# Two models' blocks on one core: modulation pieces in the index and softmax stretches, projection pieces alone beside stick-breaking, a picking product, four buffers beside near attention

## The chip, the cores and the metric

One core of a Trainium2 chip runs the whole program. The metric is the device time of one execution in microseconds. The kernel before took 2896.35 us, the median of three runs (2890.53 to 2899.73).

## The reference

Two stacks of two layers each run one after the other on 256 tokens of width 1024, all in fp32. The first stack has in each layer a gated feed-forward, a mixer of three attentions (forgetting, stick-breaking, sparse with an index) and a second feed-forward:

```python
(q_a, k_a, v_a, f_a, q_b, k_b, v_b, q_c, c_kv, q_i, k_i, w_i, gates) = jnp.split(h @ w_in, _split_points(), axis=-1)
...
merged = (g_a * (y_a.reshape(B, S, W_FOX) @ w_up_fox)
          + g_b * (y_b.reshape(B, S, W_SB) @ w_up_sb)
          + g_c * (y_c.reshape(B, S, W_DSA) @ w_up_dsa))
return merged @ w_out
```

The second stack is modulated: for each layer a vector of nine times 1024 numbers is computed from a condition `c`, and one from `c_ctx`, and shifts, scales and gates the sublayers.

```python
def adaln(cond, w, b):
    m = jax.nn.silu(cond) @ w + b
    return m.reshape(m.shape[:-1] + (N_MOD, D_MODEL))
```

Its layer 0 has neighbourhood attention ("near" in the kernel) of 8 heads over 256 tokens and 256 context tokens, its layer 1 a short convolution. The modulation needs nothing but the conditions and 2 x 1024 x 9216 weights (`mod_w`, 75 MB), so it can be computed at any time before the second stack.

## The kernel before

The program is a list of phases that every engine walks through in the same order. Weights come in units of 1 MB into a ring of three buffers `raw`; ACT copies each to `whi` in a reduced format (L415), DVE subtracts to get the rest `wlo` (L428, for some units GpSimd takes 896 of 2048 columns, L670), and TensorE (PE) makes three products for each block: `whi` x `HThi`, `whi` x `HTlo`, `wlo` x `HThi`.

In a layer of the first stack the mixer runs as the phases prepare, latent, turn_index, index (top-k rounds on DVE), softmax (22 items, one for each head and block of queries) and stick (5 heads, a chain through all engines: scores z, logs, sums acc, weights, values pv). Their own work leaves engines idle, and so other work is laid beside it, cut in pieces (class `Beside`, L444). A string `BESIDE` (L42) gives the order of the pieces and `PACE` (L44) how many each phase does at each of its calls of `beside.go`. Every engine walks through the same string and does its share of each piece:

- D, a quarter of a weight unit of the remaining projections of `w_in`: on PE 6 matmuls of 512 columns (`part`, L737); on ACT the split of a later unit, and for the last D of a group of eight two evacuations (L1139, copy or tanh); on DVE, at each fourth D, the `wlo` split of a unit two ahead (L1428).
- m, 256 columns of the modulation: SP loads 1 MB of `mod_w` as two halves (L601), PE makes 8 matmuls with the 32 columns of `CT` (both conditions 16 times over) as weights into four strips of 32 partitions of one bank (`mod`, L752), DVE copies the 128 x 256 sums to `mrow` (L1432).
- t, the turn of that row: PE transposes `mrow` in two blocks (L763), DVE adds the four strips (L1440) and the bias and writes `modc` (L1441).

The two halves land in two buffers, halves of the tile `C`, so a half may be loaded when the previous row's same half has been used (`s_mod_used`). In the first stack sums and turn share bank 5, so m waits until DVE has read the previous turn (`row_read`). Beside near attention (16 items of 512 columns, phase near) the banks are 6 and 7. Of the 72 rows, 26 are computed in each of the two layers of the first stack and 20 beside near.

The stick phase on PE, with the calls of pieces after each head's step:

```python
for h in range(HS + 2):
    if h < HS:
        z(h)
    if 1 <= h <= HS:
        acc(h - 1)
    if h >= 2:
        pv(h - 2)
    beside.go(beside.pace["stick"])
```

Of the kernel before, what the change touches and what calls it, by code (L numbers as in the profile page):

```python
# [6 lines left out]
ALU = mybir.AluOpType  # L7
# [34 lines left out]
BESIDE = ("mDDDDDDDDt" * 4 + "mDtDmDtDmDtDmDtD" * 5 + "mDtDmDDDtDDD",) * 2 + ("m" + "tm" * 19 + "t",)  # L42

PACE = (dict(prepare=8, latent=(4, 2), turn_index=3, index=(4, 4, 4, 4, 4, 3), softmax=4, item=(2,), stick=6),) * 2 + (dict(item=(2, 2, 3)),)  # L44
# [7 lines left out]
def constants():  # L52
# [11 lines left out]
    add("ident", np.eye(P))  # L64
    add("upto", i[:, None] <= i[None, :])
# [40 lines left out]
def program(nc, t, out):  # L106
    with ExitStack() as ctx:
# [31 lines left out]
        mraw = C[:].rearrange("p b (c n) -> p b c n", c=4)  # L139
# [77 lines left out]
        def pieces(order, w=None, groups=()):  # L217

            out, part, groups = [], 0, iter(groups)
            for what in order:  # L220
# [10 lines left out]
                elif what == "m":  # L231
                    layer, column = next(mods)
                    out.append(("mod", len(mod_units)))
                    mod_units.extend(kn(t["mod_w_2"][layer], 4 * half, 4, column, MOD) for half in range(2))
                else:
                    out.append(("turn", layer, column // P))
            return out

        for l in range(DEPTH):
# [5 lines left out]
            def projected(n0, n1, *more):  # L245
# [7 lines left out]
            phase("beside", first=len(units), pieces=pieces(BESIDE[l], w, later), pace=PACE[l], end=len(units), banks=(5, 5),  # L253
                  after=0 if l == 0 else c_read)
# [31 lines left out]
        for l in range(DEPTH):  # L286
# [6 lines left out]
            if l == 0:  # L293
# [10 lines left out]
                phase("beside", first=len(units), pieces=pieces(BESIDE[2]), pace=PACE[2], end=len(units), banks=(6, 7), after=c_read)  # L304
# [24 lines left out]
        s_mod, s_mod_used = [sem(f"mod_landed{h}") for h in range(2)], sem("mod_used")  # L329
# [239 lines left out]
        four = small[:, 494:498].rearrange("p (k s) -> p k s", s=2)  # L569
# [6 lines left out]
        def _(sp):  # L576
# [24 lines left out]
            def load_mod(m):  # L601
                if m >= 2:
                    sp.wait_ge(s_mod_used, m - 1)
                sp.dma_start(mraw[:, m % 2], mod_units[m]).then_inc(s_mod[m % 2], 16)
# [15 lines left out]
            for ph in phases:  # L620
# [19 lines left out]
                elif ph["kind"] == "beside":  # L640
# [4 lines left out]
                    for what, m, *p in ph["pieces"]:  # L645
                        if what == "part" and p[1] == 0:
                            begin(m + 2)
                        elif what == "mod":
                            load_mod(m)
# [52 lines left out]
        def _(pe):  # L702
# [49 lines left out]
            def mod(m):  # L752
# [3 lines left out]
                for half in range(2):  # L756
                    pe.wait_ge(s_mod[half], 16 * (m // 2 + 1))
                    for c in range(4):
                        i = mm(ps[32 * c:32 * c + 32, total, 0:MOD], CT[:, 4 * half + c, :], mraw[:, half, c, :],
# [3 lines left out]
            def turn_row(l, k0):  # L763
# [3 lines left out]
                for k in range(MOD // P):  # L767
                    i = nc.tensor.transpose(ps[:, turned, k * P:(k + 1) * P], mrow[:, k * P:(k + 1) * P], ident)  # L768
# [1059 lines left out]
```

## Time and profile before

| | |
|---|---|
| median of 3 runs | 2896.35 us |
| the profiled execution, its time | 2887.4 us |
| its span (first to last instruction) | 2885.6 us |
| PE busy | 2668.5 us, 92% |
| DVE, ACT busy | 1417.5 us (49%), 1174.3 us (41%) |
| DMA | 496.16 MB, mean 172 GB/s |
| mean granted clock of TensorE | 0.952 of 2.4 GHz |

The profile is of one execution. Busy time of PE is a modelled span of pipelined matmuls. A granted clock of 1.00 is 2.4 GHz, 0.50 is 1.2 GHz. A wait names the engine and line that released it. Some fp32 matmul instructions of the program stand as two in the trace; transposes stand as one.

### The profile page before, as it was taken

Reading aid. Unit: us, or ns where it says so; the run is one execution under the profiler, and the core shown is the slowest. Engines: PE = TensorE matmul, PEld = TensorE weight load, DVE = VectorE, ACT = ScalarE, POOL = GpSimd, SP = SyncE. Lnnn points to the kernel's source line nnn. Section 1 sums busy time; section 2 is a strip of 40 time slices with the busy share of each in tenths; the row PEclk is TensorE's granted clock in tenths of the full one; section 3 lists DMA queues with packets and bytes.
Section 4 is the critical chain, followed back from the end, with each engine's and each line's share of the span. In section 5 each row is a group of like instructions: output and inputs, shape, how many; then the busy total and the mean of one; then the engine's idle time right before and its main releaser. Section 6 shows DMA issues by size and latency. Waiting matters only on the chain.

```text
span 2885.6 us, 34246 instructions
## 1 busy us (share of the span) xinstructions
PE 2668.5 (92%) x12829; PEld 2112.8 (73%) x12829; DVE 1417.5 (49%) x1830; ACT 1174.3 (41%) x1356; POOL 111.4 (4%) x85
## 2 busy tenths in 40 slices
PE   7998988899999898889989989978889999998998
PEld 6886655688788765568878878865567878876786
DVE  4555334645555633465554455543335455455554
ACT  4435333444443433444443443443024444444433
POOL 0002110000000211000000000020000000000000
PEclk9999999999999999999989999987789999998999
DMA  6555564465555656455545545562454545554453
GB/s 210 189 163 198 175 208 157 151 194 184 168 183 178 200 175 196 160 177 191 187 134 187 189 141 184 185 146 97 157 173 162 187 155 192 187 166 131 157 188 114
DMA packets 367783, 496.16 MB, mean 172 GB/s; under 512 B 14478, under 2 KB 295338, under 8 KB 367562
## 3 DMA queue, kind: packets, MB, share of 16 engines
q1 hardware_dynamic: 365338, 487.99, 51.8%
q0 software_dynamic: 2064, 5.84, 1.1%
q8 instruction: 64, 1.05, 0.1%
q10 hardware_dynamic: 288, 1.05, 0.1%
q14 instruction: 29, 0.24, 0.0%
HBM read 493.77 MB, written 1.05 MB: 171 GB/s over the span
## 4 chain that ended last, share of the span: by engine, by line
PE 84%; DVE 7%; ACT 4%; DMA 3%; issue 1%; DVEq 0%; ACTq 0%; SPq 0%; PEldq 0%
PE ps L706 79%; PE ps L786 2%; DVE wlo L428 2%; PE ps L905 2%; DMA C<-in_mod_w_dram 1%; ACT whi L415 1%; DMA raw<-in_even_w_in_dram 1%; PE ps L793 1%; PE ps L768 1%; ACT L1315 0%; DVE arena L1469 0%; DMA raw<-in_even_w_out_dram 0%; DVEq L348 0%; ACT work L1156 0%; PE ps L876 0%
## 5 line engine op out<-in xcount | busy, mean ns | idle before, releaser
L428 DVE TENSOR_TENSOR wlo<-raw,whi 128x2048 fp32r<-128x2048 f32 (+5 forms) x405 | 872.0, 2155 | 606.7 <-ACT whi L415 604.5
L706 PE MATMUL ps<-whi,HThi 128*128 128x512 f32 (+2 forms) x2360 | 958.1, 406 | 38.6 <-DVE HTlo L1475 16.9
L415 ACT ACTIVATE whi<-raw 128x2048 fp32r<-128x2048 f32 (+4 forms) x405 | 752.7, 1861 | 467.1 <-PE ps L706 432.8
L706 PE MATMUL ps<-whi,HTlo 128*128 128x512 f32 (+2 forms) x2360 | 932.8, 395 | 0.0
L706 PE MATMUL ps<-wlo,HThi 128*128 128x512 f32 (+2 forms) x2360 | 932.8, 395 | 0.0
L706 PEld LDWEIGHTS ps<-whi,HThi 128*128 128x128 f32 x2360 | 452.6, 192 | 162.5 <-issue 50.8
L706 PEld LDWEIGHTS ps<-wlo,HThi 128*128 128x128 f32 x2360 | 452.6, 192 | 96.9
L706 PEld LDWEIGHTS ps<-whi,HTlo 128*128 128x128 f32 x2360 | 453.5, 192 | 85.4
L706 PE MATMUL ps<-whi,AThi 128*128 128x512 f32 x792 | 310.0, 391 | 1.1
L706 PE MATMUL ps<-wlo,AThi 128*128 128x512 f32 x792 | 308.5, 390 | 0.0
L706 PE MATMUL ps<-whi,ATlo 128*128 128x512 f32 x792 | 308.2, 389 | 0.0
L1225 ACT ACTIVATE AThi<-ps 128x512 fp32r<-128x512 f32 x99 | 59.1, 597 | 291.9 <-PE ps L905 291.9
L706 PEld LDWEIGHTS ps<-whi,AThi 128*128 128x128 f32 x792 | 148.7, 188 | 34.9 <-issue 4.7
L706 PEld LDWEIGHTS ps<-wlo,AThi 128*128 128x128 f32 x792 | 148.6, 188 | 31.1
L706 PEld LDWEIGHTS ps<-whi,ATlo 128*128 128x128 f32 x792 | 148.7, 188 | 30.2
L1537 DVE TENSOR_TENSOR ATlo<-ps,AThi 128x512 fp32r<-128x512 f32 x99 | 68.4, 691 | 155.5 <-ACT AThi L1225 155.5
L706 PE MATMUL ps<-C,CT 128*32 128x256 f32 x1152 | 95.5, 453 | 42.6 <-DVE modc L1441 26.7
L1132 ACT ACTIVATE work<-ps,small 128x128 f32<-128x128 f32 (+2 forms) x60 | 29.5, 492 | 219.7 <-DVE small L1391 219.5
L1221 ACT ACTIVATE arena<-ps 128x256 f32<-128x256 f32 x110 | 36.2, 381 | 186.5 <-PE ps L706 186.5
L670 POOL TENSOR_TENSOR wlo<-raw,whi 128x896 fp32r<-128x896 f32 x36 | 84.0, 2333 | 390.6 <-ACT whi L415 390.6
L1221 ACT ACTIVATE arena<-ps,small 128x256 f32<-128x256 f32 x88 | 36.9, 470 | 140.8 <-PE ps L706 140.7
L1390 DVE TENSOR_REDUCE small<-ps 128x1 f32<-128x128 f32 (+2 forms) x60 | 26.8, 447 | 133.5 <-PE ps L786 87.8
(191 smaller groups left out, 1593.0 us busy)
## 6 DMA issues: line engine op xcount, KB each, us to landing
raw<-in_ffn_w_dram SPq DMA_DIRECT2D x330, 512.0 KB, 4.2
raw<-in_w_ffn_gu_dram SPq DMA_DIRECT2D x176, 512.0 KB, 4.6
C<-in_mod_w_dram SPq DMA_DIRECT2D x144, 512.0 KB, 4.3
raw<-in_w_ffn_down_dram SPq DMA_DIRECT2D x88, 512.0 KB, 4.0
raw<-in_w_in_dram SPq DMA_DIRECT2D x40, 1024.0 KB, 7.3
raw<-in_even_w_in_dram SPq DMA_DIRECT2D x12, 1024.0 KB, 5.1
raw<-in_conv_w_in_dram SPq DMA_DIRECT2D x12, 1024.0 KB, 5.1
raw<-in_w_out_dram SPq DMA_DIRECT2D x8, 1024.0 KB, 5.0
```

The source lines that it names most:

```text
L415: i = nc.scalar.activation(whi[0:rows, r, a:b], raw[0:rows, r, a:b], ACT.Copy)
L428: i = nc.vector.tensor_tensor(wlo[0:rows, r, a:b], raw[0:rows, r, a:b], whi[0:rows, r, a:b].bitcast(F32), ALU.subtract)
L670: nc.gpsimd.tensor_tensor(wlo[at], raw[at], whi[at].bitcast(F32), ALU.subtract).then_inc(s_lo_pool, 1)
L706: return nc.tensor.matmul(o, lhsT, rhs, start=first, stop=last)
L768: i = nc.tensor.transpose(ps[:, turned, k * P:(k + 1) * P], mrow[:, k * P:(k + 1) * P], ident)
L786: i = nc.tensor.matmul(S[:, o:o + ow], lh, rh, start=False, stop=j == len(mine) - 1)
L793: i = nc.tensor.transpose(T[:, c * P:(c + 1) * P], prob[(n - 1) % 2][:, c * P:(c + 1) * P], ident)
L905: i = nc.tensor.transpose(ps[:, 2, c * SEQ + b * P:c * SEQ + (b + 1) * P], av[:, b, c * P:(c + 1) * P], ident)
L1132: A(prob[n % 2][:, 0:it["n"]], ps[:, n % 2, 0:it["n"]], ACT.Exp, bias=nmx[:, n:n + 1], scale=SCALE, accum_out=rsum[:, n:n + 1]).then_inc(s ...
L1221: A(sg[:, b, :], ps[:, b, 0:GW], ACT.Silu, scale=scale).then_inc(sem("ffn_silu"), 1)
L1225: A(AT[own][0][:], ps[:, 2, :].rearrange("p (c t) -> p c t", c=2), ACT.Copy).then_inc(sem("ffn_act_hi"), 1)
L1537: V.tensor_tensor(AT[own][1][:], ps[:, 2, :].rearrange("p (c t) -> p c t", c=2), AT[own][0][:].bitcast(F32), ALU.subtract).then_inc(sem("f ...
```

## The change

`BESIDE` becomes `PROJECT + GATE`: up to the end of the index phase 32 D, 9 m and 9 t (before 32, 4 and 4, then two D, an m and a t ahead of the first item, now three D, an m and a t), in the 24 steps of softmax 24 D, 16 m, 16 t (before 24, 12, 12), and in stick 21 D alone (before 22 D, 9 m, 9 t). The turn is no longer two transposes but two products of `mrow` as weights with a constant of two columns, `pick`, which has a one in column s at the rows s of each strip of 32. They add the strips on PE and leave 4 columns, so that DVE only adds the bias, and reads 4 columns of PSUM. Beside near, four buffers are used in turn, two of them in `arena` where the matrices of the pooling branch lie until the phase near_turn is over: SP waits for that phase on PE before it loads them (`late`). Three pieces (m, t, m) come ahead of the first near item, and then two to each item.

```diff
@@ -39,9 +39,11 @@
 PJ_LATER = ((902, 1414), (1414, 1926), (390, 902), (0, 390))
-BESIDE = ("mDDDDDDDDt" * 4 + "mDtDmDtDmDtDmDtD" * 5 + "mDtDmDDDtDDD",) * 2 + ("m" + "tm" * 19 + "t",)
-
-PACE = (dict(prepare=8, latent=(4, 2), turn_index=3, index=(4, 4, 4, 4, 4, 3), softmax=4, item=(2,), stick=6),) * 2 + (dict(item=(2, 2, 3)),)
+PROJECT = "DDDDDDDm" + "tDDm" + "DD" + "tDm" + "tDDDm" * 6 + "tDD"
+GATE = "mDtDD" + "mDtDmtD" * 8 + "D" * 21
+BESIDE = (PROJECT + GATE,) * 2 + ("mtm" + "tm" * 18 + "t",)
+
+PACE = (dict(prepare=8, latent=(4, 2), turn_index=3, index=(5, 5, 5, 5, 5, 8), softmax=5, item=(2, 3, 2), stick=3),) * 2 + (dict(near=3, item=(2,)),)
 MOD = 256
@@ -62,6 +64,7 @@
     add("ident", np.eye(P))
+    add("pick", i[:, None] % 32 == np.arange(2)[None, :])
     add("upto", i[:, None] <= i[None, :])
@@ -136,7 +139,8 @@
         CT = sb("CT", [P, DC, 32])
-        mraw = C[:].rearrange("p b (c n) -> p b c n", c=4)
+        mraw = [C[:, b, :].rearrange("p (c n) -> p c n", c=4) for b in range(NB)]
+        mraw += [arena[:, at:at + 1024].rearrange("p (c n) -> p c n", c=4) for at in (3072, 4096)]
         mrow = work[:, 3072:3072 + MOD]
@@ -214,7 +218,7 @@
 
-        def pieces(order, w=None, groups=()):
+        def pieces(order, bufs, w=None, groups=()):
 
@@ -230,8 +234,10 @@
                     layer, column = next(mods)
-                    out.append(("mod", len(mod_units)))
-                    mod_units.extend(kn(t["mod_w_2"][layer], 4 * half, 4, column, MOD) for half in range(2))
+                    base = len(mod_units)
+                    out.append(("mod", base))
+                    mod_units.extend((kn(t["mod_w_2"][layer], 4 * half, 4, column, MOD), bufs[(base + half) % len(bufs)])
+                                     for half in range(2))
                 else:
@@ -250,8 +256,8 @@
                       for n0 in range(0, 3 * D, 512)]
-            phase("beside", first=len(units), pieces=pieces(BESIDE[l], w, later), pace=PACE[l], end=len(units), banks=(5, 5),
-                  after=0 if l == 0 else c_read)
+            phase("beside", first=len(units), pieces=pieces(BESIDE[l], mraw[0:2], w, later), pace=PACE[l], end=len(units), banks=(5, 5),
+                  after=0 if l == 0 else c_read, late=0)
             for kind in ("prepare", "latent", "turn_index", "index", "softmax", "stick"):
@@ -301,7 +307,7 @@
                 phase("near_turn")
-                phase("beside", first=len(units), pieces=pieces(BESIDE[2]), pace=PACE[2], end=len(units), banks=(6, 7), after=c_read)
+                phase("beside", first=len(units), pieces=pieces(BESIDE[2], mraw), pace=PACE[2], end=len(units), banks=(6, 7), after=c_read, late=len(phases))
                 phase("near")
@@ -326,7 +332,7 @@
         s_lo, s_lo_pool = sem("unit_lo"), sem("unit_lo_by_pool")
-        s_mod, s_mod_used = [sem(f"mod_landed{h}") for h in range(2)], sem("mod_used")
+        s_mod, s_mod_used = [sem(f"mod_landed{h}") for h in range(4)], sem("mod_used")
 
@@ -566,7 +572,6 @@
         gB = GT.rearrange("p b n -> p (b n)")[:, 4096:5120]
-        four = small[:, 494:498].rearrange("p (k s) -> p k s", s=2)
         half_rstd = small[:, 498:500]
@@ -599,9 +604,10 @@
             def load_mod(m):
-                if m >= 2:
-                    sp.wait_ge(s_mod_used, m - 1)
-                sp.dma_start(mraw[:, m % 2], mod_units[m]).then_inc(s_mod[m % 2], 16)
+                (src, buf), before = mod_units[m], [k for k in range(m) if mod_units[k][1] is mod_units[m][1]]
+                if before:
+                    sp.wait_ge(s_mod_used, before[-1] + 1)
+                sp.dma_start(buf, src).then_inc(s_mod[mraw.index(buf)], 16)
 
@@ -646,6 +652,8 @@
                         elif what == "mod":
+                            if mod_units[m][1] is mraw[2] and ph["late"]:
+                                sp.wait_ge(sem("phases_pe"), ph["late"])
                             load_mod(m)
@@ -754,9 +762,10 @@
                 for half in range(2):
-                    pe.wait_ge(s_mod[half], 16 * (m // 2 + 1))
+                    buf = mod_units[m + half][1]
+                    pe.wait_ge(s_mod[mraw.index(buf)], 16 * sum(o is buf for _, o in mod_units[:m + half + 1]))
                     for c in range(4):
-                        i = mm(ps[32 * c:32 * c + 32, total, 0:MOD], CT[:, 4 * half + c, :], mraw[:, half, c, :],
+                        i = mm(ps[32 * c:32 * c + 32, total, 0:MOD], CT[:, 4 * half + c, :], buf[:, c, :],
                                half == 0, half == 1)
@@ -765,7 +774,7 @@
                 for k in range(MOD // P):
-                    i = nc.tensor.transpose(ps[:, turned, k * P:(k + 1) * P], mrow[:, k * P:(k + 1) * P], ident)
+                    i = mm(ps[:, turned, 2 * k:2 * k + 2], mrow[:, k * P:(k + 1) * P], cc("pick"))
                 i.then_inc(sem("row_turned"), 1)
@@ -975,7 +984,7 @@
                 kind = ph["kind"]
-                if kind in ("latent", "turn_index", "softmax"):
+                if kind in ("latent", "turn_index", "softmax", "near"):
                     beside.go(ahead(beside.pace, kind))
@@ -1181,7 +1190,7 @@
                 split.upto(first_unit[n] + RING - 1 if n else 0)
-                if kind in ("latent", "turn_index", "softmax"):
+                if kind in ("latent", "turn_index", "softmax", "near"):
                     beside.go(ahead(beside.pace, kind))
@@ -1436,9 +1445,7 @@
                 r, nk = VEC_ROWS["mod_b"] + l * NMOD * DC + k0, MOD // P
-                rows = ps[:, beside.banks[1], 0:MOD].rearrange("p (k m r) -> p k r m", k=nk, m=4)
-                link(V.tensor_reduce(four, rows[:, :, 0:2, :], AX_X, ALU.add))
-                V.tensor_tensor(modc[:, l, k0:k0 + nk, :], four,
+                V.tensor_tensor(modc[:, l, k0:k0 + nk, :], ps[:, beside.banks[1], 0:2 * nk].rearrange("p (k s) -> p k s", s=2),
                                 vec[:, r:r + nk].unsqueeze(2).broadcast_to([P, nk, 2]), ALU.add).then_inc(sem("row_read"), 1)
@@ -1485,7 +1492,7 @@
                 split.upto(first_unit[n] + RING - 1 if n else 0)
-                if kind in ("latent", "turn_index", "softmax"):
+                if kind in ("latent", "turn_index", "softmax", "near"):
                     beside.go(ahead(beside.pace, kind))
```

The last edit, "near" in the list of kinds, stands in ACT's and DVE's loops too.

On DVE, one step of stick-breaking in layer 0, first before. L1723 to L1737 are the head's own work, `mod_used` and `row_turned` are signals from PE, `stick_L`, `stick_exp` from ACT.

```order
L1723 TENSOR_SCALAR work<-ps 128x384 [waits stick_L]
L1724 TENSOR_TENSOR work<-work 128x384 [waits dve_chain]
L1725 SCALAR_TENSOR_TENSOR work<-ps,work 128x384 [waits dve_chain]
L1726 TENSOR_TENSOR work<-work,cst 128x128 [waits dve_chain]
L1727 TENSOR_TENSOR work<-work,cst 128x128
L1734 TENSOR_TENSOR work<-ps,work 128x384 [waits stick_acc]
L1736 TENSOR_TENSOR work<-work,cst 128x128 [waits stick_exp]
L1737 TENSOR_TENSOR work<-work,cst 128x128
L1434 COPY work<-ps 128x256 [waits mod_used]
L1440 TENSOR_REDUCE small<-ps 128x4 [waits row_turned]
L1441 TENSOR_TENSOR modc<-small,vec 128x4 [waits dve_chain]
L1434 COPY work<-ps 128x256 [waits mod_used]
```

Now the same step:

```order
L1730 TENSOR_SCALAR work<-ps 128x384 [waits stick_L]
L1731 TENSOR_TENSOR work<-work 128x384 [waits dve_chain]
L1732 SCALAR_TENSOR_TENSOR work<-ps,work 128x384 [waits dve_chain]
L1733 TENSOR_TENSOR work<-work,cst 128x128 [waits dve_chain]
L1734 TENSOR_TENSOR work<-work,cst 128x128
L1741 TENSOR_TENSOR work<-ps,work 128x384 [waits stick_acc]
L1743 TENSOR_TENSOR work<-work,cst 128x128 [waits stick_exp]
L1744 TENSOR_TENSOR work<-work,cst 128x128
L434 TENSOR_TENSOR wlo<-raw,whi 128x1152 [waits unit_hi]
```

Between the head's work and the next head's there is only the split of a weight unit (L428, now L434).

On DVE, a part of the top-k rounds in the index phase (MAX and MATCH_REPLACE), before:

```order
L1674 MAX small<-work 128x8 [waits index_step0]
L1674 MAX small<-work 128x8 [waits index_step1]
L1677 MATCH_REPLACE work<-small,work 128x128 [waits index_step0]
L1677 MATCH_REPLACE work<-small,work 128x256 [waits index_step1]
L1674 MAX small<-work 128x8 [waits index_step0]
L1674 MAX small<-work 128x8 [waits index_step1]
L1677 MATCH_REPLACE work<-small,work 128x128 [waits index_step0]
L1677 MATCH_REPLACE work<-small,work 128x256 [waits index_step1]
L1440 TENSOR_REDUCE small<-ps 128x4 [waits row_turned]
L1441 TENSOR_TENSOR modc<-small,vec 128x4 [waits dve_chain]
L1434 COPY work<-ps 128x256 [waits mod_used]
```

And now:

```order
L1681 MAX small<-work 128x8 [waits index_step0]
L1681 MAX small<-work 128x8 [waits index_step1]
L1684 MATCH_REPLACE work<-small,work 128x128 [waits index_step0]
L1684 MATCH_REPLACE work<-small,work 128x256 [waits index_step1]
L1448 TENSOR_TENSOR modc<-ps,vec 128x4 [waits row_turned]
L434 TENSOR_TENSOR wlo<-raw,whi 128x1152 [waits unit_hi]
L1443 COPY work<-ps 128x256 [waits mod_used]
L1681 MAX small<-work 128x8 [waits index_step0]
L1681 MAX small<-work 128x8 [waits index_step1]
L1684 MATCH_REPLACE work<-small,work 128x128 [waits index_step0]
L1684 MATCH_REPLACE work<-small,work 128x256 [waits index_step1]
```

A turned row, a split and the copy of the next row's sums now stand between every two pairs of rounds, where before a row's two operations came with every second or third pair.

On PE, the start of near attention, before. `ps<-C,CT` are the modulation's matmuls (two halves), L786 and the rows around it are an item's scores.

```order
L706 MATMUL ps<-work 128x256 [waits pool_split,pooled_copied] x2
L706 MATMUL ps<-arena 128x256 [waits pool_split,phases_dve,phases_act,near_in]
L786 MATMUL ps<-arena,cst 128x256
L786 MATMUL ps<-cst 128x256
L706 MATMUL ps<-arena 128x256
L706 MATMUL ps<-C,CT 32x256 [waits mod_landed0]
L706 MATMUL ps<-C,CT 32x256 x3
L706 MATMUL ps<-C,CT 32x256 [waits mod_landed1]
L706 MATMUL ps<-C,CT 32x256 x3
L768 MATMUL ps<-cst,work 128x128 [waits row_copied]
L768 MATMUL ps<-cst,work 128x128
L706 MATMUL ps<-arena 128x256
```

And now (scores start with the last row):

```order
L714 MATMUL ps<-work 128x256 [waits pool_split,pooled_copied] x2
L714 MATMUL ps<-C,CT 32x256 [waits pool_split,phases_dve,phases_act,mod_landed0]
L714 MATMUL ps<-C,CT 32x256 x3
L714 MATMUL ps<-C,CT 32x256 [waits mod_landed1]
L714 MATMUL ps<-C,CT 32x256 x3
L714 MATMUL ps<-cst,work 128x2 [waits row_copied]
L714 MATMUL ps<-cst,work 128x2
L714 MATMUL ps<-arena,CT 32x256 [waits mod_landed2]
L714 MATMUL ps<-arena,CT 32x256 x3
L714 MATMUL ps<-arena,CT 32x256 [waits mod_landed3]
L714 MATMUL ps<-arena,CT 32x256 x3
L714 MATMUL ps<-arena 128x256 [waits near_in,phases_dve,phases_act]
```

The scores of the first item now stand behind two modulations and a turn, and the second modulation reads the new buffers.

## Rows read from the trace of the kernel before

**Rows 1.** Windows: us, busy us of each engine (instructions), granted clock, DMA share, GB/s.

```profile
237.10:309.50 72.40, 64.63 (x363) 50.29 (x363) 41.78 (x136) 32.79 (x52) 17.05 (x7) 0.93 0.50 168
309.50:399.90 90.40, 90.00 (x573) 60.01 (x572) 35.91 (x115) 27.25 (x57) 10.50 (x6) 1.00 0.63 209
399.90:484.80 84.90, 64.46 (x385) 44.00 (x385) 31.33 (x76) 35.17 (x42) 8.39 (x4) 0.90 0.54 179
...
1123.60:1210.80 87.20, 66.53 (x384) 45.53 (x384) 31.32 (x76) 35.17 (x42) 7.50 (x4) 0.84 0.54 174
```

**Rows 2.** PE's waits in stick-breaking, layer 0: total, times, longest.

```profile
PE ps L706 <- DVE modc L1441: 9.6, 2, 5.7
PE ps L768 <- DVE work L1434: 8.5, 3, 3.2
```

**Rows 3.** Timeline of one stick-breaking step: start, us, engine, line, operation.

```profile
427.31 0.92 PE L706 MATMUL ps<-arena 64*128 64x256 f32 x4
427.42 1.26 ACT L1147 ACTIVATE arena<-ps,small 128x512 f32<-128x512 f32 x2 [6.13 <-PE ps L706]
...
428.58 0.49 ACT L1313 ACTIVATE work<-ps 128x384 f32<-128x384 f32 x1
...
429.87 1.07 PE L706 MATMUL ps<-C,CT 128*32 128x256 f32 x16
...
431.53 0.56 DVE L1723 TENSOR_SCALAR work<-ps 128x384 f32<-128x384 f32 x1 [4.28 <-ACTq L1316]
...
434.31 0.52 ACT L1322 ACTIVATE work<-work 128x384 f32<-128x384 f32 x1 [1.47 <-DVE work L1734]
434.74 1.89 ACT L415 ACTIVATE whi<-raw 128x2048 fp32r<-128x2048 f32 x1
```

**Rows 4.** PE's waits beside near attention, 1993.4 to 2131.7.

```profile
PE ps L706 <- DMA C<-in_mod_w_dram: 11.0, 9, 2.2
PE ps L768 <- DVE work L1434: 6.9, 11, 0.6
```

**Rows 5.** Windows of near attention, columns as in rows 1.

```profile
1993.40:2131.70 138.30, 120.27 (x680) 68.76 (x680) 39.95 (x110) 13.73 (x33) 0.00 (x0) 0.72 0.48 156
1993.40:2034.00 40.60, 36.15 (x150) 18.75 (x150) 8.93 (x24) 4.39 (x9) 0.00 (x0) 0.50 0.33 104
2064.80:2085.20 20.40, 19.88 (x92) 11.22 (x85) 5.40 (x14) 1.55 (x4) 0.00 (x0) 0.50 0.37 114
```

**Rows 6.** Timeline of PE in the softmax stretch.

```profile
326.93 1.07 PE L706 MATMUL ps<-C,CT 128*32 128x256 f32 x16
327.93 0.50 PE L706 MATMUL ps<-whi,HThi 128*128 128x512 f32 x1
...
329.52 0.70 PE L706 MATMUL ps<-arena 64*128 64x256 f32 x2
...
331.75 0.39 PE L768 MATMUL ps<-cst,work 128*128 128x128 f32 x2
331.89 0.48 PE L706 MATMUL ps<-whi,HThi 128*128 128x512 f32 x1
```

**Rows 7.** Timeline of PE: the only matmuls with few columns.

```profile
302.18 0.80 PE L706 MATMUL ps<-small,cst 128*128 128x6 f32 x6 [1.45 <-ACT arena L1113]
```

**Rows 8.** PE's wait for a turned row in the index stretch.

```profile
PE ps L706 <- DVE modc L1441: 3.6, 3, 2.3
```

**Rows 9.** Timeline of PE beside near attention.

```profile
2037.68 1.07 PE L706 MATMUL ps<-C,CT 128*32 128x256 f32 x16
...
2042.65 0.64 PE L706 MATMUL ps<-C,CT 128*32 128x256 f32 x8
2043.48 0.42 PE L706 MATMUL ps<-C,CT 128*32 128x256 f32 x4 [0.18 <-DMA C<-in_mod_w_dram]
```

**Rows 10.** DMA issues, KB, median us to landing: softmax stretch, then near.

```profile
C<-in_mod_w_dram SPq DMA_DIRECT2D x24, 512.0 KB, 4.5
...
C<-in_mod_w_dram SPq DMA_DIRECT2D x38, 512.0 KB, 3.7
```

## The prediction

> **What bounds the kernel now.** I first cut the span into the stretches that the change touches and read TensorE's busy time and granted clock in each [rows 1]. Outside them nothing moves. In the softmax stretch PE is busy for 90.00 of 90.40 us at full clock: every microsecond of PE work added there is a microsecond of time. In the index stretch it is busy for 64.63 of 72.40, and in stick-breaking for only 64.46 of 84.90 (66.53 of 87.20 in layer 1). Near attention takes 138.30 us at a mean clock of 0.72 [rows 5]. So time is to be had in two places, stick-breaking and near, and it is spent in the other two.
>
> Then I asked for what PE waits in stick-breaking [rows 2]: 9.6 us for the finished turn of a modulation row (L1441) and 8.5 us for the copy of a row (L1434), both on DVE; one wait is 5.7 us. DVE is not busy then. Its instructions stand in order, and the row pieces stand behind the chain of the head: ACT runs Abs, Exp, a table load and Ln, DVE only then gets its first work of the step, after 4.28 us idle, and the head's weights are not through Exp before 434.83 [rows 3]. PE stands at a modulation piece meanwhile, and the next head's scores are behind it, so ACT starts its next Abs late too. The starved chain and the starved PE feed each other.
>
> Near attention has two faults. PE waits 11.0 us for modulation data and 6.9 us in 11 waits for a row copy [rows 4]. And it is at 1.2 GHz (0.50) for 40.60 us at the start and 20.40 us later [rows 5]; a mean of 0.72 is (1 - 0.72) x 2 x 138.30 = 77 us at half clock in all, which cost 38.
>
> **The change, part by part.** A modulation piece is 1.00 us of PE (start to start), a projection piece 1.6, and a turn by two transposes only 0.14, since the next matmuls start at once behind it [rows 6].
>
> *The picking product.* An fp32 matmul takes two instructions per call: three calls with 6 columns stand as x6 and take 0.80 us, so 0.11 between starts once the last one's drain is off [rows 7]. A turn is now four of these, 0.44 instead of 0.14: +0.3 us on PE wherever PE is the bound. Bounds: 0 (hidden by a wait) and 0.6 (from 0.80 for six, drain in it). DVE loses a reduction, a hop of 0.2 us that nobody waits for once stick-breaking is rid of rows.
>
> *Index stretch.* It gets 5 more modulation pieces (+5.0), one more projection piece (+1.6) and 10 turns at 0.44 for 5 at 0.14 (+3.7). In the new order a turn stands directly behind its modulation eight or so times, so PE waits for DVE's copy, 0.6 us each (6.9/11) [rows 4]: +5.0. Against it, 3.6 us of waits for L1441 [rows 8] mostly go, since three projection pieces now stand between a turn and the next modulation: -3. Sum +12. Bounds +7 (the waits are filled) and +18 (DVE, which also has the top-k rounds, is late each time by 1 us more).
>
> *Softmax stretch.* 24 projection pieces as before, 16 modulations for 12 (+4.0), turns 16 x 0.44 - 12 x 0.14 (+5.4). Sum +9.4, with no cover. The copies are covered by the projection or the item that now stands between a modulation and its turn.
>
> *Loads.* With two buffers the next row's second half can be asked for 1.0 us after the present one starts. In near, rows at an interval of 4.97 us waited 0.18 us for that half [rows 9], so two buffers carry an interval of about 5.2 with nothing else on the queue. The new intervals are 1.0 + 0.44 + 3 x 1.6 + 0.6 = 6.8 in index and (90.4 + 9.4)/16 = 6.2 in softmax. That is enough, but the median landing was 4.5 us in softmax against 3.7 in near [rows 10], as the 1 MB units share the queue. I take 0 for stalls, with 0 to 10 us a layer as bounds.
>
> *Stick-breaking.* Nine modulations and nine turns leave; 21 projection pieces stay for 22. They need from DVE only a wlo split, due two units ahead, so nothing on PE waits for DVE but the head's own steps. Now the step is ACT's: from Abs to the end of Exp 6.25 us (428.58 to 434.83), then a split of 1.89 in most steps and an evacuation of 1.26 in three of five [rows 3]: 6.25 + 1.6 + 0.8 = 8.7. PE needs 2.6 for the head (427.31 to 429.87) [rows 3] and 4.8 for three pieces, 7.4, so it fits under it. Five steps are 43, about 1 before the first and 7 behind the last (two products, the values, three projection pieces): 51. I add 3 for idle gaps of some 2 us that still cost clock: 54 for 84.90, -31; in layer 1 -33. From below, PE's own work (5 x 2.6 + 21 x 1.6 = 47) allows -38. From above, if the evacuations and PE's pieces keep the two in lock-step, one step is 8.7 + 4.8 = 13.5 and the gain is about 16.
>
> *A layer* is then +12 + 9.4 - 32 = -10.6, both -21.
>
> *Near.* Four buffers: each item now has one turn and one modulation, the turn belongs to the row of the item before, and data is asked for two rows ahead. The waits for data and copies go: -17.9. With 20 turns of +0.3: +6. The start costs: PE's second modulation now stands before the first scores, and its two halves may be asked for only when near_turn is through on PE. They need 3.7 us to land and some more for the second half, and the two modulations and a turn run at half clock: first scores 6 us later than now, +6 (bounds 4 and 9). The clock: it starts low all the same. The spells at half clock were 40.6, 20.4 and 16 us in shorter ones, and of the later ones I hold the waits for data guilty, which are gone. I take one of 25 us, between the second and the first, which costs 12.5 for 38: -26. Sum -32, of which I take -30. An independent count: 6 + 16 items x 5.3 + 6.5 behind the last + 12.5 = 110 for 138.3.
>
> **Sum.** -21 - 30 = -51 us. The profiled execution took 2887.4 us, so it would take 2836. It lay 9 us (0.3%) under the median of 2896.35, and against that the forecast is **2845 us**. About 0.3%, 8.7 us, is what a measurement of this kernel can tell from no change.
>
> **Rivals.**
> (a) *The loads turn on it, and it gets slower.* 25 rows of a layer now come in index and softmax at 6.2 to 6.8 us, where softmax has 24 halves, 12 rows, in 90.4 us now, 7.5 each [rows 1, 10]. If a unit gets in front of a row each time, the row lands 2 us later and PE stalls about 1.5 us, 50 times: +75, so 2920. It decides from 1.0 us per row, where the whole gain of 51 is gone. For it speaks that 4.5 us against 3.7; against it that a unit is issued behind a row's halves in SP's order, and that softmax moves 209 GB/s now [rows 1] and would need 231 (four more rows of 1.05 MB in 99.8 us). The Trainium skill (DMA: Bandwidth & Descriptors, Latency and other measured facts) gives 0.2 us on average but 2 us at high load for HBM's latency, which would be this case; the median landings differ by 0.8 us only. 7%.
> (b) *Near stays at half clock.* A wait of some 3 us stands at its start, and an item at half clock takes nearly twice the 4.97 + 0.3 of [rows 9], about 9.5: 16 x 9.5 + 6 + 10 = 168, +30 for -30, so 2905. Both long spells ended by themselves under the same instructions [rows 5]. 8%.
> (c) *Stick-breaking gains half*, by the lock-step above: -16 a layer instead of -32, 2877. 13%.
> (d) *Near is soon at full clock*, and PE's own work bounds stick-breaking sooner: 10 to 15 us more, 2832. The Trainium skill (TensorE: Matmul & The Clock Gate, Part 4) says that the fast clock does not engage for transposes, as they do not count as busy in the same way. By that rule products in their place help. No row here tells transposes and products apart in this, and the sum has nothing of it. 10%.
> (e) The forecast: 62%, by itself 2822 to 2866.
>
> **How the numbers follow.** (c), (d) and (e) are faster by over 8.7 us: 85%. (a) and (b) are split between slower and unchanged, as each may come in part: 8% slower, 7% unchanged. The range takes in (e), (d) and (c) with a margin: 2818 to 2882; outside it are (a), (b) and the ends of the others.
>
> **What would show it.** Stick-breaking within 50 to 58 us, with no PE wait on the row instructions and ACT's Abs starts some 9 us apart; softmax 98 to 101 us at PE busy 99%; index 82 to 86 with eight or more waits of 0.6 for the row copy; near 100 to 115 with no wait for data but the one at its start. Waits of PE for mod_w data in softmax would speak for (a); softmax over 105 or stick-breaking over 65 would make the step wrong.

## The result, and the profile after

The changed kernel takes 2919.43 us, the median of six runs (2912.94 to 2924.76); the kernel before took 2891.78 in six (2884.05 to 2899.73). The ratio is 1.0106, with a 95% interval of 1.0086 to 1.0125: slower by 1.1%. The forecast was 2845, with a range of 2818 to 2882. The profiled execution took 2924.6 us, 37.2 more than the one of before, and its span was 2921.6.

Two lines of the profile's page, busy time by engine and the granted clock of 40 slices in tenths:

```profile
PE 2721.5 (93%) x12973; PEld 2160.4 (74%) x12973; DVE 1407.8 (48%) x1758; ACT 1174.4 (40%) x1356; POOL 110.2 (4%) x85
...
PEclk9999998999999999899999999987569999998999
```

PE is busy for 53 us more than before (2668.5), and there is a 5 where near attention lies, in a slice in which the page of before has a 7.

I put the two traces side by side by the instructions that both have (scores, sums, products of the heads) and read the stretches between them. Windows of the changed kernel, columns as in [rows 1]: index from its first turn, softmax and stick-breaking of layer 0; softmax and stick-breaking of layer 1; near from its first scores, and its parts by clock:

```profile
252.24:326.29 74.05, 62.65 (x421) 45.77 (x421) 32.18 (x110) 26.24 (x39) 10.48 (x5) 0.98 0.68 226
326.29:429.27 102.98, 99.71 (x676) 65.95 (x676) 36.49 (x111) 27.24 (x57) 12.47 (x6) 1.00 0.69 230
429.27:491.63 62.36, 50.17 (x216) 40.02 (x217) 27.10 (x49) 35.06 (x42) 7.61 (x3) 0.84 0.22 75
...
1056.02:1159.80 103.78, 101.61 (x677) 67.34 (x676) 36.55 (x111) 27.25 (x57) 12.48 (x6) 0.98 0.69 227
1159.80:1222.87 63.07, 50.83 (x216) 40.52 (x217) 27.09 (x49) 35.07 (x42) 7.61 (x3) 0.82 0.24 73
2011.05:2168.52 157.47, 156.27 (x694) 100.23 (x690) 37.25 (x90) 13.73 (x33) 0.00 (x0) 0.52 0.40 128
...
2005.00:2162.00 157.00, 155.91 (x667) 98.14 (x667) 35.70 (x85) 13.73 (x33) 0.00 (x0) 0.50 0.39 124
2162.00:2168.50 6.50, 5.30 (x60) 4.01 (x60) 2.13 (x7) 0.00 (x0) 0.00 (x0) 1.00 1.02 333
```

Beside [rows 1] and [rows 5] this gives, in us:

| stretch | forecast | layer 0 | layer 1 |
|---|---|---|---|
| index | +12 | +15.1 | +17.3 |
| softmax | +9.4 | +12.6 | +13.5 |
| stick-breaking | -31, -33 | -22.5 | -24.2 |
| layer | -10.6 | +5.1 | +6.7 |

(Each is the shift of the stretch's last instruction less that of its first, 1.7 us at the start of layer 0 and 5.4 at that of layer 1.) So the layers give +12 for -21. Of the 33 us between, stick-breaking has 17, index 8 and softmax 7. Near, from the last products before it to its end, gives +22.6 for -30 (the shift is 11.9 us there and 34.5 behind). Near now runs at 1.2 GHz for 157 us in one piece, from its opening into its tail, although PE is busy for 155.91 of them. One item of it, PE's timeline (start, us, engine, line, operation):

```profile
2032.82 0.96 PE L714 MATMUL ps<-cst,work 128*128 128x2 f32 x4
2033.71 1.93 PE L714 MATMUL ps<-C,CT 128*32 128x256 f32 x16
2035.57 1.22 PE L714 MATMUL ps<-arena 64*128 64x256 f32 x2
2036.72 1.22 PE L795 MATMUL ps<-arena,cst 128*128 128x256 f32 x2
2037.73 1.06 PE L795 MATMUL ps<-cst 128*128 128x256 f32 x2
2038.73 1.22 PE L714 MATMUL ps<-arena 64*128 64x256 f32 x2
2039.88 1.11 PE L802 MATMUL ps<-cst,work 128*128 128x128 f32 x4
2040.79 1.80 PE L714 MATMUL ps<-arena,work 128*128 128x64 f32 x8
2042.38 0.96 PE L714 MATMUL ps<-cst,work 128*128 128x2 f32 x4
```

The waits that the change was to take away are gone: from the turn at 2032.82 to the next at 2042.38 nothing stands between the groups. The 9.56 us of an item are all work at half speed. The first and last rows are the picking products, 128x2.

PE's waits in the changed kernel, for index, softmax and stick-breaking of layer 0 in turn (waited for, us, times, longest):

```profile
PE ps L714 <- DVE work L1443: 4.4, 7, 1.1
PE ps L714 <- ACT arena L1158: 2.7, 2, 1.4
...
PE ps L714 <- DVE modc L1448: 0.7, 1, 0.7
...
PE ps L714 <- DMA C<-in_mod_w_dram: 3.0, 4, 1.7
...
PE ps L714 <- ACT arena L1156: 10.1, 2, 5.6
```

### The profile page after: what moved, and what is told of

The parts are those of the page before. It is cut to its first block, busy times and chain, and to the rows that moved or that the text cites. A ratio compares the mean times of both kernels' runs of the same rounds, so it can differ in the third digit from the quotient of the medians.

```text
span 2921.6 us, 34471 instructions
## 1 busy us (share of the span) xinstructions
PE 2721.5 (93%) x12973; PEld 2160.4 (74%) x12973; DVE 1407.8 (48%) x1758; ACT 1174.4 (40%) x1356; POOL 110.2 (4%) x85
## 4 chain that ended last, share of the span: by engine, by line
PE 85%; DVE 6%; DMA 3%; ACT 3%; issue 1%; ACTq 0%; DVEq 0%; SPq 0%; PEldq 0%
PE ps L714 80%; PE ps L795 2%; DMA C<-in_mod_w_dram 2%; PE ps L914 2%; DVE wlo L434 1%; ACT whi L421 1%; DMA raw<-in_even_w_in_dram 1%; PE ps L802 1%; DVE arena L1476 0%; ACTq L354 0%; DMA raw<-in_even_w_out_dram 0%; ACT work L1165 0%; PE ps L885 0%; DVE HTlo L1368 0%; ACT L1324 0%
## 5 line engine op out<-in xcount | busy, mean ns | idle before, releaser
L434 DVE TENSOR_TENSOR wlo<-raw,whi 128x2048 fp32r<-128x2048 f32 (+5 forms) x405 | 870.9, 2152 | 608.1 <-ACT whi L421 606.4
L1443 DVE COPY work<-ps 128x256 f32<-128x256 f32 x72 | 30.6, 424 | 125.9 <-PE ps L714 125.9
```

The lines of the kernel that those rows point to most:

```text
L434: i = nc.vector.tensor_tensor(wlo[0:rows, r, a:b], raw[0:rows, r, a:b], whi[0:rows, r, a:b].bitcast(F32), ALU.subtract)
L1443: V.tensor_copy(mrow, ps[:, beside.banks[0], 0:MOD]).then_inc(sem("row_copied"), 1)
```

## The experiments

The questions were: what holds near at half clock (the picking products, the even order, the buffers), what the picking product costs in the layers, and where stick-breaking's missing 9 us a layer are.

**Transposes again, everywhere.** The edit, with DVE's old reduction:

```diff
-                    i = mm(ps[:, turned, 2 * k:2 * k + 2], mrow[:, k * P:(k + 1) * P], cc("pick"))
+                    i = nc.tensor.transpose(ps[:, turned, k * P:(k + 1) * P], mrow[:, k * P:(k + 1) * P], ident)
```

> The changed kernel with the old turn (two transposes on PE, reduction on DVE) everywhere. In the changed kernel near attention ran at 1.2 GHz for 157 us in one piece, without gaps. Theory P (the picking products, 2 columns each, in place of transposes keep TensorE at half clock there): near returns to a mean clock of 0.75 or more and to 100 to 125 us, for 162; with 0.3 us less per turn for 52 turns in the layers (-16), about 2860 us. Theory O (the even order, one turn and one row to each item, keeps it low): near stays at half clock and is 157 us, 2900. Theory S (the opening of three pieces with its wait starts the low spell, and it would have ended by chance): between the two. In the layers the picking product's price is tested too: I say -16 us in both together, and if it is hidden there, 0.

Measured: 2846.28 us, ratio to the kernel before 0.983 (0.9794 to 0.9865). Near, in the columns of [rows 5]:

```profile
1996.44:2089.06 92.62, 90.05 (x656) 55.52 (x653) 39.36 (x109) 13.74 (x33) 0.00 (x0) 0.92 0.66 217
```

With nothing else altered but DVE's reduction, near falls from 157.5 to 92.6 us and comes to a mean clock of 0.92. Theory P holds, and near is even under its 100 to 125 us; theory O is out.

**Transposes beside near alone.** The edit: the same, under `if total != turned`.

> The changed kernel with the old turn beside near attention alone. Theory P: near 100 to 125 us, total about 2875. Theory O: near 157 us, total 2914. The layers as in the changed kernel (+12 against the kernel before), so that the difference from the kernel with transposes everywhere is the picking product's price in the layers.

Measured: 2861.41 us, ratio 0.9869 (0.9833 to 0.9905), near 91.60 us. The same effect on near, and 15 us between this and the kernel above: the picking product's price in the layers, 0.29 us for each of the 52 turns. The stretches of one execution of each show it less evenly (softmax 105.71 for 98.99 us in layer 0, with a spell at half clock in it), and the two intervals overlap, so the size is rough. Both near and the total (2875 expected) came out lower than theory P had them.

**The pace as before, with picking products.** The edit: `dict(item=(2, 2, 3))` for `dict(near=3, item=(2,))`, and "near" out of the lists of kinds.

> The changed kernel with picking products and four buffers, but the pace beside near as before: no pieces ahead of the first item, then 2, 2 and 3 pieces by turns. Theory P: near stays at half clock nearly throughout, 155 to 165 us, 2915 to 2920. Theory O or S: the clock rises as before, near 125 to 138 us, 2885 to 2895.

Measured: 2908.22 us, median of ten runs that lie from 2866.65 to 2934.85. The ratio is 0.9955 (0.9912 to 0.9997) by the six runs up to 2908.91, and 1.004 by the median of all ten. Near of the profiled execution, then two parts of it:

```profile
2005.29:2150.78 145.49, 137.53 (x725) 88.21 (x726) 37.53 (x92) 13.74 (x33) 0.00 (x0) 0.64 0.49 159
...
2010.00:2040.00 30.00, 27.53 (x224) 18.10 (x216) 11.22 (x28) 5.95 (x13) 0.00 (x0) 1.00 0.65 212
2042.00:2112.00 70.00, 67.45 (x293) 42.55 (x291) 15.68 (x37) 5.45 (x14) 0.00 (x0) 0.50 0.34 110
```

Neither of my two numbers. Behind 3.4 us at half in the first item the clock is full here for 30 us, with picking products in every item, through three waits of 0.6 us for the row's copy. Within a microsecond of the fourth it falls, at 2040.2, and is at half for nearly all the rest. PE's timeline there, with a turn at full clock before it:

```profile
2032.19 0.56 PE L714 MATMUL ps<-cst,work 128*128 128x2 f32 x4
2032.68 1.07 PE L714 MATMUL ps<-arena,CT 128*32 128x256 f32 x16
...
2039.53 0.58 PE L714 MATMUL ps<-cst,work 128*128 128x2 f32 x4 [0.64 <-DVE work L1443]
2040.04 1.06 PE L714 MATMUL ps<-arena 64*128 64x256 f32 x2
```

In the profile of the changed kernel's order the clock came back only in the last 6.5 us, and its six runs lie within 12 us; with the old order the runs spread over 68 us. So with picking products the order has a part in what the clock does, and the rest varies from run to run.

**The kernel before with the picking product.** The edit, with DVE's reduction left out:

```diff
-                    i = nc.tensor.transpose(ps[:, turned, k * P:(k + 1) * P], mrow[:, k * P:(k + 1) * P], ident)
+                    i = mm(ps[:, turned, 2 * k:2 * k + 2], mrow[:, k * P:(k + 1) * P], cc("pick"))
```

> The kernel before with the picking product in place of the transposes, nothing else. Theory P: near falls to half clock nearly throughout and is 155 us or more, +20; the layers +0.3 for each turn where PE is busy (12 in each softmax stretch, 5 in each index stretch: +7 to +10 in all): 2920. Theory O or S: near +3, total 2900 to 2905.

Measured: 2934.61 us, ratio 1.0133 (1.0097 to 1.017). Near:

```profile
2006.39:2180.58 174.19, 157.25 (x725) 98.74 (x726) 37.84 (x92) 13.73 (x33) 0.00 (x0) 0.56 0.40 128
```

174.19 us at 0.56, for 140.64 in the same bounds before. Theory P predicted this from the other side, with the old buffers and the old order, though near grew by 34 us for its 20. The layers grew by 16.5 us for its 7 to 10, as +3.0 and +3.2 in the softmax stretches (12 turns each: 0.26 a turn), +2.9 and -0.2 in index, and +4.2 and +3.5 in stick-breaking, where I had expected nothing.

**A full product in place of the transpose, beside near.** Is it that these are products, or that they have two columns?

```diff
-                        i = nc.tensor.transpose(ps[:, turned, k * P:(k + 1) * P], mrow[:, k * P:(k + 1) * P], ident)
+                        i = mm(ps[:, turned, k * P:(k + 1) * P], mrow[:, k * P:(k + 1) * P], ident)
```

> Against the kernel with transposes everywhere (2846 us, near attention 92.6 us at 14.1 us of half clock), with one edit: beside near, mrow is turned by an ordinary product with the identity, 128 columns, instead of a transpose (DVE reduces as with the transpose). Theory C (the two columns are the fault: a turn that streams few columns lets the engine count as less busy): the clock rises as with transposes, near 93 to 105 us, total 2850 to 2860. Theory M (products of this kind as such keep it low, transposes do not): near at half clock throughout, 160 us or more, total 2910 or more.

Measured: 2841.64 us (two runs), ratio 0.9831 (0.9799 to 0.9864). Near as a whole, its opening at half clock and the stretch behind that, then its turn in PE's timeline:

```profile
1997.74:2092.04 94.30, 92.21 (x693) 60.36 (x690) 39.35 (x109) 13.73 (x33) 0.00 (x0) 0.96 0.65 215
1991.70:2005.40 13.70, 12.84 (x65) 5.98 (x66) 2.58 (x9) 2.06 (x3) 0.00 (x0) 0.50 0.71 230
2005.40:2092.00 86.60, 84.51 (x661) 56.28 (x661) 37.53 (x104) 11.67 (x30) 0.00 (x0) 1.00 0.66 216
```

```profile
2013.20 0.66 PE L715 MATMUL ps<-cst,work 128*128 128x128 f32 x4
```

The same four instructions with the same weights, 128 columns for 2, and the clock rises after 13.7 us and stays. Near is as theory C has it, the total 8 us under its range. Products as such are not the fault; the two columns are. (DVE's reduction goes with the 128 columns in every run, so no run separates these two; but behind the opening of the changed kernel's near PE has only two waits left, of 0.6 us each and in its tail.) At full clock the turn now takes 0.59 us to the next start (2013.79). The pick took 0.49 before the same kind of matmuls (2032.19 to 2032.68 above), and 0.42 in the changed kernel's softmax stretch:

```profile
336.60 0.56 PE L714 MATMUL ps<-cst,work 128*128 128x2 f32 x4
337.02 0.48 PE L714 MATMUL ps<-whi,HThi 128*128 128x512 f32 x1
```

So 126 useless columns cost 0.10 us a turn beside near, and leaving them out costs 63 us of near.

**No turn on PE beside near.** Left out: the modulation of the 20 rows there (modc gets the bias alone).

```diff
                 take("row_copied")
+                if total != turned:
+                    return
```

> As the kernel with transposes everywhere, but beside near no row is turned on PE at all: PE only waits for the row's copy, DVE writes the bias alone into modc, so the modulation of these 20 rows is left out. If the picking products hold the clock down by being there, near without them is at full clock soon: 85 to 95 us. If the transposes are what lifts it, near without either stays at half clock: 9.2 us an item, 150 us.

Measured: 2840.73 us (two runs), ratio 0.9828 (0.9809 to 0.9848), near 87.41 us at 0.92. Transposes are not needed to lift the clock. The clock rises without any turn, and beside near it is the short products' presence that keeps it down. That is no rule for every stretch: in the changed kernel's softmax stretches 16 such turns stand between projections of 512 columns, and the clock is 1.00 and 0.98; and in near's tail three stand behind the rise at 2162.

**Another pace in stick-breaking**, on the kernel with transposes everywhere:

```diff
-softmax=5, item=(2, 3, 2), stick=3),) * 2
+softmax=5, item=(2, 3, 2), stick=(2, 3, 4, 4, 2, 3, 3)),) * 2
...
-                        beside.go(beside.pace["stick"])
+                        beside.go(beside.pace["stick"][h])
```

> As the kernel with transposes everywhere, but in stick-breaking the seven steps do 2, 3, 4, 4, 2, 3 and 3 projection pieces in place of 3 each, so that the pieces that end a group of eight (the 5th, 13th and 21st) stand last in a step, and the next head's scores and sums stand between them and the piece that waits for ACT's evacuation of the group. Theory V (the two PE waits of 4.5 and 5.6 us for that evacuation, and the half clock behind them, are what the forecast of 54 us for the stretch missed): stick-breaking 54 to 58 us in each layer for 60.7 and 62.4, total 2834 to 2841. Rival (the chain of the head on ACT is the bound whatever the pieces do, the waits only move): 60 to 63, total 2846.

Measured: 2822.29 us, ratio 0.9778 (0.9752 to 0.9804). Stick-breaking in both layers:

```profile
424.80:475.42 50.62, 42.93 (x216) 34.57 (x217) 25.29 (x49) 34.64 (x42) 9.90 (x3) 1.00 0.28 91
1134.52:1185.18 50.66, 44.32 (x217) 35.90 (x217) 25.29 (x49) 34.62 (x42) 9.89 (x3) 0.97 0.30 95
```

PE's waits for ACT in the first of them, where it was 10.1 for two in the changed kernel:

```profile
PE ps L715 <- ACT arena L1160: 1.7, 2, 1.0
```

The same 21 projection pieces take 10 and 12 us less, more than theory V asked for. The clock stays up as well, 1.00 and 0.97 for 0.86 and 0.83. (The ratios' intervals, 0.9752 to 0.9804 and 0.9794 to 0.9865, just touch; the gain is read from the stretches.) This is the stretch as the forecast had drawn it, and even 3 us under its 54.

**Two buffers beside near, with transposes.** The edit: `pieces(BESIDE[2], mraw[0:2])`.

> As the kernel with transposes everywhere, but with two buffers beside near instead of four. Theory B (the four buffers take away the waits for data, 11.0 us before, and with them the half clock): near 110 us or more, data waits of 10 us or more, total 2862 or more. Rival (the order of one turn and one row to each item and the opening do it; two buffers carry an interval of 5.3 us as they carried 4.97): near 93 to 97, total 2846 to 2850.

Measured: 2863.4 us, ratio 0.9889 (0.9858 to 0.9921). Near and its wait for data:

```profile
2000.94:2116.14 115.20, 107.19 (x656) 62.27 (x652) 39.60 (x109) 13.75 (x33) 0.00 (x0) 0.78 0.56 181
```

```profile
PE ps L715 <- DMA C<-in_mod_w_dram: 6.5, 7, 1.6
```

Near is 115.2 us as theory B has it, the data waits are 6.5 where I had asked for 10 or more. They and the half clock around them (0.78 for 0.92) cost 22.6 us in this execution, the slowest of four that lie from 2848.07 to 2868.26.

**Four buffers, the pace as before, transposes.** The edit as in the third experiment.

> As the kernel with transposes everywhere (2846 us, near 92.6 us), with four buffers but the pace beside near as before (nothing ahead of the first item, then 2, 2 and 3 pieces by turns). Theory B (buffers): near 92 to 100, data waits under 3 us, total 2840 to 2853. Theory O (the pace): two rows in every third item bring back data waits and row copy waits (6.9 us before), and with them the half clock: near 115 to 138, 2870 to 2890.

Measured: 2845.3 us, ratio 0.9856 (0.9817 to 0.9895). Near and PE's wait for the row's copy:

```profile
1988.40:2100.26 111.86, 103.53 (x686) 61.72 (x687) 40.43 (x112) 13.73 (x33) 0.00 (x0) 0.84 0.61 199
```

```profile
PE ps L779 <- DVE work L1447: 6.9, 11, 0.6
```

There is no wait for data, but the 6.9 us of row copies are those of [rows 4] to a tenth. The profiled near lies between the two theories' ranges, nearer to O's, and the median in B's. The runs spread over 23 us, so in the time this one is not settled; in the profile each of the two edits takes away its own wait, and both are needed for 92 us. Behind the rise the clock stays up here, through eight of the waits for a row's copy:

```profile
2028.00:2096.00 68.00, 62.89 (x503) 39.85 (x504) 29.60 (x82) 9.33 (x24) 0.00 (x0) 1.00 0.67 217
```

The order, the buffers and these waits are those of the third experiment, where with picking products the clock fell in the fourth such wait and stayed low. So the picking products do not only hold a low clock down: in these two executions they also go with the loss of a high one.

**The near part alone.** The kernel before with four buffers, `near=3, item=(2,)` and transposes.

> The kernel before with the near part of the change alone: four buffers, three pieces ahead of the first item and two to each, the turn by transposes. If the parts add up, near is 92 to 95 us for 140.6 and nothing else moves: 2892 - 47 = 2845, the same as with the layers' part too (2846), so that the layers' part with its stick pace of 3 is worth 0 to 3 us. Rival (the layers' part and transposes are worth more, near less): above 2855.

Measured: 2850.22 us, ratio 0.9875 (0.9859 to 0.9892). Near:

```profile
2008.43:2101.19 92.76, 90.15 (x655) 55.45 (x652) 39.33 (x109) 13.74 (x33) 0.00 (x0) 0.92 0.67 217
```

Near gives the same 92.8 us by itself, and the total lies between the 2845 and the 2855 of the two theories. The layers' part, with transposes and its stick pace of 3, is then worth what lies between 0.9875 and 0.983, some 13 us with intervals that overlap; in single executions it was 3 us. A single execution is a rough measure of this: ahead of near the two kernels have the same code, and yet this execution stands 9.4 us behind that of the kernel before when near begins.

**The index order**, on the version with the new stick pace:

```diff
-PROJECT = "DDDDDDDm" + "tDDm" + "DD" + "tDm" + "tDDDm" * 6 + "tDD"
+PROJECT = "DDDDDDDm" + "DtDm" + "DD" + "tDm" + "DtDDm" * 6 + "DtD"
```

> As the kernel with transposes and the stick pace 2, 3, 4, 4, 2, 3, 3 (2822 us), with one edit: up to the end of the index stretch a projection piece stands between each modulation and its turn (DtDDm for tDDDm). Theory W (PE's waits for the row's copy directly behind a modulation, 6.1 us in 7 waits in layer 0, are what the index stretch pays beyond its PE work): the index stretch 4 to 6 us shorter in each layer, for 73.2 and 72.1, total 2810 to 2814. Rival (ACT's and DVE's own index work is late anyway and PE only waits elsewhere): within 2 us a layer, 2818 to 2822.

Measured: 2817.52 us, ratio 0.976 (0.9743 to 0.9777). The wait for the row's copy fell as meant, from 4.4 us in 7 waits to this:

```profile
PE ps L779 <- DVE work L1447: 1.1, 1, 1.1
```

The index stretch got shorter by 3.8 us in layer 0 and 1.6 in layer 1, less than theory W's 4 to 6, at a clock of 0.95 where it was 0.98 in layer 0, and stick-breaking took 53.2 and 53.7 us for 50.6. The total is above theory W's 2810 to 2814 and just under the rival's 2818. The two versions can't be told apart (0.976 and 0.9778, overlapping intervals). Both beat the kernel before, by 2.2 and 2.4%, and so the changed one too.

## Why the prediction was wrong, by its steps

**Near's clock is the step that failed.** The forecast said "I take one spell of 25 us", and -30 for near. The spell was 157 us and near +22.6: 53 of the 85 us between forecast (-51) and outcome (+34 in the profiled stretches). The cause lies in a step that I had costed by its time alone, the picking product (+0.3 us a turn). Its time was right and its effect on the clock missing. Four experiments show it, by near's time: transposes for it 92.6 us (157.5 with it), a full product 94.3, no turn 87.4, and in the kernel before it turned 140.6 into 174.2. Rival (b) had the size (16 x 9.5 + 6 + 10 = 168 for a measured 163.5 from the opening) but named the wait at the start as the reason, which every version with transposes has as well. By its own reason it should not have come true.

Rival (d) drew on the Trainium skill (TensorE: Matmul & The Clock Gate, Part 4), which says that the fast clock does not engage for transposes. That products in their place should help was the forecast's own conclusion. No run here has a stretch of transposes alone; in near's mixed stream the conclusion is wrong, with a mean clock of 0.92 with transposes and 0.52 with these products.

**Near's other terms held.** Data and row copy waits went as said: none is left after the opening. The start cost 6 us as said (788.2 us from the end of stick-breaking in layer 1 to near's first scores, for 782.5). With transposes the half clock behind the first scores is 14 us, shorter than my 25, and near gains 48 us, 42 with its opening, where I had 30.

**Softmax: PE's work right, the loads not nothing.** PE busy rose from 90.0 to 99.7 us, +9.7 for my +9.4. On top came waits for mod_w data, 3.0 us in layer 0 and 1.8 in layer 1, which I had taken as 0 with bounds of 0 to 10. In layer 1 a spell of half clock that begins 4.8 us before the stretch's end made up the rest. Rival (a), 1.5 us at each of 50 rows, did not come.

**Index: a wait that I had not named.** The waits for the row's copy came to 4.4 us in 7 (my 5.0 in 8), the one for a turned row fell to 0.7 from 3.6 [rows 8] (my -3), and PE's busy time rose by 10.4 (75.05 us from 238.70 to the first scores, for 64.63; my 10.3). The 3 us that are missing in layer 0 are PE's waits for ACT's evacuation at L1158, 3.9 us in three where one of 0.9 stood before. The 2 us more in layer 1 are PE's busy time: from the first turn on it was 49.3 us there before, for 50.7 in layer 0 (clock 0.97 and 0.94), and is now 62.9 and 62.7 (0.98 in both).

**Stick-breaking: "it fits under it" failed.** The row waits went, but a projection piece that begins a group must wait for ACT to evacuate the last group (L1156), and that stands behind the head's Exp. PE then stood for 4.5 and 5.6 us, the first time with the next head's scores behind it. ACT's and PE's timeline of the first of the two:

```profile
438.99 0.53 ACT L1324 ACTIVATE work<-work 128x384 f32<-128x384 f32 x1
439.20 0.39 PE L714 MATMUL ps<-wlo,HThi 128*128 128x512 f32 x1
...
442.36 0.52 ACT L1331 ACTIVATE work<-work 128x384 f32<-128x384 f32 x1 [1.47 <-DVE work L1741]
442.79 1.25 ACT L1156 ACTIVATE arena<-ps,small 128x512 f32<-128x512 f32 x2
...
444.09 0.79 PE L714 MATMUL ps<-whi,HThi 128*128 128x512 f32 x1 [4.50 <-ACT arena L1156]
```

That is the lock-step of rival (c) in two of the steps, not in all: 12.6 us between scores in one, and the clock fell during each (0.84 and 0.82 in the stretch). The forecast's bound for that rival does not add up: five steps of 13.5 and the 8 us around them are 75.5, a gain of 9 us and not 16. The pace experiment, which only moves the ends of the groups to the ends of steps, gave 50.6 us. The forecast's 54 was attainable, but not with 3 pieces in every step.

The version with transposes everywhere ran at 2846, which is nearly the forecast of 2845. That is chance: in its profiled execution near is 12 us better than I had it (-42 for -30) and the layers are 18 us worse (-3 for -21).

## What to carry over

Price a replacement by what it does to the clock of its stretch too, not only by its own time: two products of 2 columns, four instructions, in every item cost 0.5 us an item at full clock and over 60 us of near by the clock, and a wider product that computes more than is needed was the cheaper one. When a piece of side work shares an accumulator with the next, put the piece that ends the group last in a step, so that the main chain's work stands between it and the piece that needs the bank back. And when a change bundles a new instruction with a new order, run the one without the other first: here the new order and buffers with the old instruction were worth 1.7%, and the instruction lost all of it and 1.1% more.

## What the runs showed of the hardware

PE can be busy for 155.91 of 157.00 us and still be granted 1.2 GHz throughout. The same stretch with each turn as products of 128 columns in place of 2, with transposes, or with no turn at all, is at 2.4 GHz again 14 to 21 us after the clock fell at its opening. A turn by two fp32 transposes of 128 columns costs PE 0.14 us between starts in softmax [rows 6], by two picking products of 2 columns, four instructions, 0.42. The version with 128 columns has the same four weight loads, so the loads alone are not the reason; why few columns have this effect no run here shows. Nor does one tell why the clock stays full with them in softmax (16 turns in 103 us, 1.00) and falls with them beside near. Where the order is less even the same products leave the clock to chance: ten runs of one kernel lay between 2866.65 and 2934.85 us.
